# Operands of TensorE given their own start offset in SBUF for each stage of a two-block transformer kernel

## The chip, the cores and the metric

The kernel runs on one core of one Trainium2 chip. The metric is the device time of one execution in microseconds, the median of the runs shown.

## The reference

256 tokens with 1024 features go through three layers, each an attention mixer followed by a gated feed-forward block. All of it is float32.

```python
for i in range(DEPTH):                      # DEPTH = 2
    hn = rmsnorm(x, attn_norm[i])
    x = x + (mixer_dilated(...) if i % 2 == 0 else mixer_moba(...))   # layer A, layer B
    hn = rmsnorm(x, ffn_norm[i])
    x = x + conv_ffn(hn, ...)               # (silu(gate) * val) @ w_down, D_FF = 2816
# second_block: layer C
h = rms_norm(x, norm1_g[l])
proj = h @ w_in[l]                          # q, k, v, forget gate, conv input, pool input
x = x + concatenate([att, conv, pool]) @ w_out[l]
x = x + (silu(gate) * val) @ w_down[l]
```

Layer A has 16 heads and three dilated windows, so its QKV product is 1024 by 9216; layer B has 16 heads (1024 by 3072), layer C 8 heads with a forget gate, a depthwise convolution and a multi-scale pool beside them.

## The kernel before

Every large product is made of three products of float32r operands (a rounded format of 32 bits): each float32 operand is split into a rounded high part and the remainder, and high times high, high times low and low times high are added up in PSUM. The weights, 369 chunks of up to 128 x 1024 values, are streamed from memory in the order of use into a ring of six slots (RING = 6). For each chunk ScalarE writes the high part `w_hi` (L390, function split_hi) and VectorE the low part `w_lo` (L398, split_lo). `w_lo(c)` starts `lo_at(c)` values into its slot's buffer, which is 64 values (STAGGER) longer than a chunk.

The activations are split in the same way: `xg` holds eight tiles of 256 high and 256 low values for the normed input (L483 on ScalarE, L495 on VectorE), `mix_hi` and `mix_lo` the output of the mixer (L984, L1043, L1123, L1156), `g_hi` and `g_lo` two buffers of the gated hidden tile (L1790, L1841).

TensorE works through this program in order:

- QKV units (unit_chunk_pe, L678 to L680; the first chunks early_chunk_pe, L612): 128 tokens of `xg` are the stationary operand and 384 columns of `w_hi` or `w_lo` the moving one; 128 x 3 such matmuls in layer B, three times as many in A, half in C (the first unit of C has 392 columns). Attention of the pair of heads before is put between them.
- output projection (out_pe, L1236 to L1238): weights stationary, 256 columns of `mix_hi` or `mix_lo` moving.
- feed-forward block (ffn_pe, 22 hidden tiles): up projection with 512 moving columns (`xg` high and low together, L430) and 256 (L432), and down projection, 256 columns of `g_hi` or `g_lo` (L1760 to L1762). Sixteen of the tiles run in a loop of eight turns with two tiles each.
- ahead of layer C six input projections (pre_pe, project_k, L416 to L418).

The order on every engine is written out by hand, and counting semaphores tie the engines together. In SBUF each buffer starts where the one before it ends, rounded up to 32 bytes; `w_raw0` starts at byte 16512 of a partition, and small unused buffers (`par_gap`, `gap`, `g_gap`, `cv_gap`) and two pairs of small ones stand between the others and so set where these start.

Of the kernel before, what the change touches and what calls it, by code (L numbers as in the profile page):

```python
# [42 lines left out]
X0 = GAINS  # L43
GAP = 24
STAGGER = 64
LO_UP, LO_DOWN = 16, 32
# [127 lines left out]
def build(nc, x_d, xa_d, stream_d, par_d, con_d, taps_d, out_d):  # L174
# [29 lines left out]
    sb("gap", [P, GAP])  # L204
# [25 lines left out]
    fg_n, fg_l = [sb(f"fg{n}", [P, 2 * HEADS_C]) for n in range(4, 6)]  # L230
# [197 lines left out]
    def project2_k(eng, c, b, k):  # L428
        s = c % RING
        nc.tensor.matmul(bank(b, 0, 2 * TOK), w_hi[s][:, k * P:(k + 1) * P], xg[:, k, :, :].rearrange("p h t -> p (h t)"),  # L430
                         start=(k == 0), stop=False, skip_group_check=True)
        last = nc.tensor.matmul(bank(b), w_lo(c)[:, k * P:(k + 1) * P], xg_hi[:, k, :], start=False,  # L432
                                stop=(k == KT - 1), skip_group_check=True)
        if k == KT - 1:
            last.then_inc(tiles, 1)

    def project2(eng, c, per, i, b):
        eng.wait_ge(w_lo_done, at(c + 1, per, i))
        for k in range(KT):
            project2_k(eng, c, b, k)  # L440

    def project_first(eng, c, b0, b1, e, lag):

        for k in range(KT + lag):
            if k < KT:
                if k == 0:
                    eng.wait_ge(w_lo_done, c + 1)
                eng.wait_ge(x_lo, KT * e + k + 1)
                project2_k(eng, c, b0, k) if e % 2 else project_k(eng, c, bank(b0), xg_hi, xg_lo, k)
            if k >= lag:  # L450
                if k == lag:
                    eng.wait_ge(w_lo_done, c + 2)
                    if e % 2:
                        eng.wait_ge(x_new, KT * (e - 1) + 4)
                project2_k(eng, c + 1, b1, k - lag) if e % 2 else project_k(eng, c + 1, bank(b1), xg_hi, xg_lo, k - lag)
        if e % 2:
            rows_pe(eng, e)
# [11 lines left out]
    def first_hi_dve(eng):  # L469
        eng.wait_ge(x_first, 16)  # L470
        nc.vector.tensor_scalar(xg_hi[:, 0, :], xT[:, 0, :], norm_gain(0, 0), None, ALU.mult).then_inc(x_hi, 1)

    def resid_act(eng, e, m):
        if e == 0:
            x_landed(eng, m)
            if m == 1:
                eng.wait_ge(x_first, 16)
                eng.wait_ge(x_hi, 1)
        else:
            eng.wait_ge(x_new, KT * (e - 1) + m + 1)  # L480
# [10 lines left out]
    def resid_dve_lo(eng, e, m):  # L491
        eng.wait_ge(x_hi, KT * e + m + 1)
        if e == 0:
            x_landed(eng, m)
        nc.vector.scalar_tensor_tensor(xg_lo[:, m, :], xT[:, m, :], norm_gain(e, m), xg_hi[:, m, :].bitcast(F32),  # L495
                                       ALU.mult, ALU.subtract).then_inc(x_lo, 1)
# [106 lines left out]
    def early_chunk_pe(eng, st, n):  # L603
# [5 lines left out]
        def term(x, part, kk, start=False, ends=False):  # L609
            k = 2 * q + kk  # L610
            for t in range(2):
                last = nc.tensor.matmul(bank(unit_bank(st, u, t), 0, UNIT), xg[:, k, x, t * P:(t + 1) * P],  # L612
                                        part[:, kk * UNIT:(kk + 1) * UNIT], start=start, stop=ends)
                if ends and t == 0:
                    last.then_inc(att[st].unit, 1)
            return last
# [27 lines left out]
    def unit_chunk_pe(eng, st, n):  # L644
# [25 lines left out]
        for kk in range(2):  # L670
            k = 2 * q + kk
            wh, wl = w_hi[s][:, kk * width:(kk + 1) * width], w_lo(c)[:, kk * width:(kk + 1) * width]
            if st < 2 and u == 0:
                eng.wait_ge(x_lo, KT * 2 * st + k + 1)
            for t in range(2):
                out = bank(unit_bank(st, u, t), 0, width)
                hi, lo = xg[:, k, 0, t * P:(t + 1) * P], xg[:, k, 1, t * P:(t + 1) * P]
                nc.tensor.matmul(out, hi, wh, start=(k == 0), stop=False)  # L678
                nc.tensor.matmul(out, hi, wl, start=False, stop=False)  # L679
                last = nc.tensor.matmul(out, lo, wh, start=False, stop=(k == KT - 1))  # L680
                if k == KT - 1 and t == 0:
                    last.then_inc(a.unit, 1)
# [295 lines left out]
    def mix_a_act(eng, pr):  # L978
        a = att[0]
        eng.wait_ge(a.pv, pr + 1)  # L980
        if joint(pr):
            unit_wait(eng, 0, joint_unit(pr), 1)
            eng.wait_ge(a.nm, 4 * (pr + 2) + 2)
        nc.scalar.activation(mix_place(mix_hi[:, pr, :]), pv_read(pr), ACT.Copy).then_inc(a.ohi, 1)  # L984
# [55 lines left out]
    def mix_act(eng, st, pr):  # L1040
        a = att[st]
        eng.wait_ge(a.pv, pr + 1)
        nc.scalar.activation(mix_hi[:, pr, :], bank(K_BANK), ACT.Copy).then_inc(a.ohi, 1)  # L1043
# [76 lines left out]
    def mix_a_dve(eng, pr):  # L1120
        a = att[0]
        eng.wait_ge(a.ohi, pr + 1)
        nc.vector.tensor_tensor(mix_place(mix_lo[:, pr, :]), pv_read(pr), mix_place(mix_hi[:, pr, :]).bitcast(F32),  # L1123
# [29 lines left out]
    def mix_dve(eng, st, pr):  # L1153
        a = att[st]
        eng.wait_ge(a.ohi, pr + 1)
        nc.vector.tensor_tensor(mix_lo[:, pr, :], bank(K_BANK), mix_hi[:, pr, :].bitcast(F32), ALU.subtract).then_inc(a.olo, 1)  # L1156
# [57 lines left out]
    def out_pe(eng, st, idx, ms=range(KT)):  # L1214
# [19 lines left out]
        for m in ms:  # L1234
            wh, wl = w_hi[s][:, m * P:(m + 1) * P], w_lo(c)[:, m * P:(m + 1) * P]
            nc.tensor.matmul(out_acc(m), wh, mix_hi[:, k, :], start=(idx == 0 and m % 2 == 0), stop=False, skip_group_check=True)  # L1236
            nc.tensor.matmul(out_acc(m), wh, mix_lo[:, k, :], start=False, stop=False, skip_group_check=True)  # L1237
            last = nc.tensor.matmul(out_acc(m), wl, mix_hi[:, k, :], start=False, stop=(idx == KT - 1), skip_group_check=True)  # L1238
# [501 lines left out]
    def ffn_pe(f):  # L1740
        e = 2 * f + 1

        def step(eng, j, per, i):
            F, b, c, cp = ffn[f], j % 2, ffn_chunk(f, j), 3 * per
            if i is not None or j < FT:
# [3 lines left out]
                else:  # L1749
                    project2(eng, c, cp, i, 2 * b)  # L1750
                    project2(eng, c + 1, cp, i, 2 * b + 1)
                c += 2
            if i is not None or j >= 2:
# [3 lines left out]
                for m in range(KT):  # L1757
                    wh, wl = w_hi[s][:, m * P:(m + 1) * P], w_lo(c)[:, m * P:(m + 1) * P]
                    first = i is None and j == 2 and m % 2 == 0
                    nc.tensor.matmul(acc(m), wh, g_hi[b][:], start=first, stop=False, skip_group_check=True)  # L1760
                    nc.tensor.matmul(acc(m), wh, g_lo[b][:], start=False, stop=False, skip_group_check=True)  # L1761
                    last = nc.tensor.matmul(acc(m), wl, g_hi[b][:], start=False, stop=True, skip_group_check=True)  # L1762
# [10 lines left out]
    def ffn_act(f):  # L1773
        def step(eng, j, per, i):
# [10 lines left out]
            if i is not None or 0 <= t < FT:  # L1785
# [4 lines left out]
                nc.scalar.activation(g_hi[t % 2][:], gated, ACT.Copy).then_inc(F.ghi, 1)  # L1790
# [17 lines left out]
    def ffn_dve(f):  # L1808
        def step(eng, j, per, i):
# [81 lines left out]
    def pre_pe(eng):  # L1891
        project_first(eng, C_PRE, PRE_BANK[0], PRE_BANK[1], 4, 1)
        for n in range(2, N_PRE):
            project(eng, C_PRE + n, 0, None, bank(PRE_BANK[n]), xg_hi, xg_lo)
# [181 lines left out]
    def pool_mix_act(eng):  # L2076
        eng.wait_ge(pool_pe, 1)
        for t in range(2):
            nc.scalar.activation(mix_hi[:, 6 + t, :], bank(Q_BANK, t * TOK), ACT.Copy,
                                 scale=par[:, PAR_PSC + t:PAR_PSC + t + 1]).then_inc(pool_hi, 1)  # L2080

    def pool_mix_dve(eng):
        eng.wait_ge(pool_hi, 2)
        for t in range(2):
            nc.vector.scalar_tensor_tensor(mix_lo[:, 6 + t, :], bank(Q_BANK, t * TOK), par[:, PAR_PSC + t:PAR_PSC + t + 1],
                                           mix_hi[:, 6 + t, :].bitcast(F32), ALU.mult, ALU.subtract).then_inc(side_lo, 1)
# [10 lines left out]
    def conv_mix_act(eng):  # L2097
        eng.wait_ge(ln_pe, 3)
        for o in range(2):
            nc.scalar.activation(mix_hi[:, 4 + o, :], bank(PW_BANK, o * TOK), ACT.Copy).then_inc(ln_act, 1)  # L2100

    def conv_mix_dve(eng):
        eng.wait_ge(ln_act, 6)
        for o in range(2):
            nc.vector.tensor_tensor(mix_lo[:, 4 + o, :], bank(PW_BANK, o * TOK), mix_hi[:, 4 + o, :].bitcast(F32),
# [317 lines left out]
```

## Time and profile before

| | us |
|---|---|
| median of 3 runs | 1039.65 |
| lowest, highest | 1039.22, 1039.83 |
| the profiled execution, its own time | 1039.65 |
| its span | 1037.8 |
| TensorE busy (matmuls) | 1032.0, 99% |
| VectorE busy | 868.2, 84% |
| ScalarE busy | 688.1, 66% |
| GpSimd busy | 354.1, 34% |

The span goes from the first to the last instruction in the trace. A matmul's own length in the trace overlaps the next matmul's, so what a matmul costs is the distance from its start to the next start, taken from the timeline. A timeline row gives start, length, engine, line, operation, what it writes and what it reads (moving operand first, then the stationary one), and the shape.

### The profile page before, as it was taken

What the parts mean: (1) busy time and instruction counts of PE and PEld (TensorE: products, weight loads), DVE (VectorE), ACT (ScalarE), POOL (GpSimd) and SP (SyncE); (2) the same over time, 40 slices, a digit from 0 to 9 for tenths busy, and PEclk for the clock granted to TensorE, in tenths of its full rate; (3) what the DMA queues carried; (4) which work ended last, traced back from release to release, by engine and by line L of the source; (5) the groups of instructions that cost most, each with busy time, mean ns of one, the idle gap of its engine ahead of it and who ended that gap; (6) DMA issues with size and microseconds to landing.
All of it is one profiled execution on the core that took longest, in us unless ns stands there. A gap on an engine that the chain in (4) does not pass through costs nothing.

```text
span 1037.8 us, 21191 instructions
## 1 busy us (share of the span) xinstructions
PE 1032.0 (99%) x7496; PEld 962.3 (93%) x7496; DVE 868.2 (84%) x1589; ACT 688.1 (66%) x1264; POOL 354.1 (34%) x370
## 2 busy tenths in 40 slices
PE   9999999999999999999999999999999999999998
PEld 8999999999999999999999899999988998999998
DVE  7877778777799988887777999988896769999886
ACT  7766777766766655576776766665686667666563
POOL 5222222112256433332111556333350015653332
PEclk9999999999999999999999999999999999999999
DMA  9654454456476665535453566656534536666651
GB/s 317 231 164 156 148 173 160 147 172 205 160 223 212 201 194 187 179 104 186 155 175 133 187 204 218 194 190 191 159 107 135 161 123 203 204 212 193 199 163 41
DMA packets 57749, 183.34 MB, mean 177 GB/s; under 512 B 6352, under 2 KB 9680, under 8 KB 57424
## 3 DMA queue, kind: packets, MB, share of 16 engines
q1 hardware_dynamic: 56816, 181.52, 54.0%
q10 hardware_dynamic: 864, 0.92, 0.3%
q8 instruction: 41, 0.67, 0.3%
q14 instruction: 28, 0.23, 0.1%
HBM read 181.36 MB, written 1.05 MB: 176 GB/s over the span
## 4 chain that ended last, share of the span: by engine, by line
PE 94%; DVE 5%; DMA 0%; issue 0%; ACT 0%; DVEq 0%
PE ps L430 20%; PE ps L432 10%; PE ps L678 10%; PE ps L680 9%; PE ps L679 9%; PE ps L1760 6%; PE ps L1762 6%; PE ps L1761 6%; DVE w_lo L398 2%; PE ps L1236 2%; PE ps L1238 2%; PE ps L1237 2%; PE ps L612 1%; PE ps L856 1%; PE ps L901 1%; PE ps L830 1%
## 5 line engine op out<-in xcount | busy, mean ns | idle before, releaser
L398 DVE TENSOR_TENSOR w_lo<-w_raw,w_hi 128x1024 fp32r<-128x1024 f32 (+2 forms) x369 | 442.0, 1214 | 32.6 <-ACT w_hi L390 31.9
L390 ACT ACTIVATE w_hi<-w_raw 128x1024 fp32r<-128x1024 f32 (+2 forms) x369 | 353.5, 972 | 125.7 <-PE ps L432 108.6
L430 PE MATMUL ps<-xg,w_hi 128*128 128x512 f32 x1056 | 364.3, 391 | 0.8 <-DVE xg L495 0.6
L432 PE MATMUL ps<-xg,w_lo 128*128 128x256 f32 x1056 | 291.7, 276 | 0.0
L430 PEld LDWEIGHTS ps<-xg,w_hi 128*128 128x128 f32 x1056 | 198.2, 188 | 41.7 <-DVE xg L495 2.9
L432 PEld LDWEIGHTS ps<-xg,w_lo 128*128 128x128 f32 x1056 | 198.2, 188 | 0.1
L1882 POOL TENSOR_TENSOR prob_t<-prob_t,qkT 128x256 f32<-128x256 f32 x63 | 104.5, 1659 | 261.8 <-ACT prob_t L1805 261.8
L678 PE MATMUL ps<-w_hi,xg 128*128 128x384 f32 (+1 forms) x556 | 192.3, 346 | 0.0
L680 PE MATMUL ps<-w_hi,xg 128*128 128x384 f32 (+1 forms) x556 | 187.4, 337 | 0.0
L679 PE MATMUL ps<-w_lo,xg 128*128 128x384 f32 (+1 forms) x556 | 185.6, 334 | 0.0
L1760 PE MATMUL ps<-g_hi,w_hi 128*128 128x256 f32 x528 | 146.2, 277 | 0.5 <-DVE g_lo L1841 0.3
L1761 PE MATMUL ps<-g_lo,w_hi 128*128 128x256 f32 x528 | 145.9, 276 | 0.0
L1762 PE MATMUL ps<-g_hi,w_lo 128*128 128x256 f32 x528 | 145.8, 276 | 0.0
L1876 POOL TENSOR_TENSOR qkT<-prob,rms_r 128x256 f32<-128x256 f32 x132 | 125.9, 974 | 18.5 <-ACT rms_r L543 10.7
L1852 DVE SCALAR_TENSOR_TENSOR qkT<-qkT,par 128x255 f32<-128x255 f32 (+1 forms) x264 | 112.3, 478 | 6.5 <-ACT qkT L1798 6.5
L1798 ACT ACTIVATE qkT<-qkT,par 128x256 f32<-128x256 f32 x132 | 78.2, 598 | 50.5 <-POOL qkT L1876 48.8
L678 PEld LDWEIGHTS ps<-w_hi,xg 128*128 128x128 f32 x556 | 104.2, 187 | 3.3 <-issue 2.7
L680 PEld LDWEIGHTS ps<-w_hi,xg 128*128 128x128 f32 x556 | 104.5, 188 | 0.0
L679 PEld LDWEIGHTS ps<-w_lo,xg 128*128 128x128 f32 x556 | 104.3, 188 | 0.1
L1760 PEld LDWEIGHTS ps<-g_hi,w_hi 128*128 128x128 f32 x528 | 99.1, 188 | 3.7 <-issue 1.3
L1762 PEld LDWEIGHTS ps<-g_hi,w_lo 128*128 128x128 f32 x528 | 99.1, 188 | 0.0
L1761 PEld LDWEIGHTS ps<-g_lo,w_hi 128*128 128x128 f32 x528 | 99.1, 188 | 0.0
(191 smaller groups left out, 1389.6 us busy)
## 6 DMA issues: line engine op xcount, KB each, us to landing
w_raw<-w_stream SPq DMA_DIRECT2D x228, 512.0 KB, 4.0
w_raw<-w_stream SPq DMA_DIRECT2D x137, 384.0 KB, 3.3
w_raw<-w_stream SPq DMA_DIRECT2D x4, 392.0 KB, 3.1
con<-consts SPq DMA_DIRECT2D x1, 1024.0 KB, 7.1
x_all<-x_t SPq DMA_DIRECT2D x4, 256.0 KB, 5.3
conv_taps<-taps SPq DMA_DIRECT2D x1, 1024.0 KB, 7.7
w_raw<-w_stream SPq DMA_DIRECT2D x4, 192.0 KB, 4.6
x_all<-x_a SPq DMA_DIRECT2D x3, 256.0 KB, 5.5
```

Of the source, the lines that this page charges most:

```text
L390: nc.scalar.activation(w_hi[s][:, 0:w], w_raw[s][:, 0:w], ACT.Copy).then_inc(w_hi_done, 1)
L398: nc.vector.tensor_tensor(w_lo(c)[:, 0:w], w_raw[s][:, 0:w], w_hi[s][:, 0:w].bitcast(F32), ALU.subtract).then_inc(w_lo_done, 1)
L430: nc.tensor.matmul(bank(b, 0, 2 * TOK), w_hi[s][:, k * P:(k + 1) * P], xg[:, k, :, :].rearrange("p h t -> p (h t)"), start=(k == 0), stop= ...
L432: last = nc.tensor.matmul(bank(b), w_lo(c)[:, k * P:(k + 1) * P], xg_hi[:, k, :], start=False, stop=(k == KT - 1), skip_group_check=True)
L678: nc.tensor.matmul(out, hi, wh, start=(k == 0), stop=False)
L679: nc.tensor.matmul(out, hi, wl, start=False, stop=False)
L680: last = nc.tensor.matmul(out, lo, wh, start=False, stop=(k == KT - 1))
L1760: nc.tensor.matmul(acc(m), wh, g_hi[b][:], start=first, stop=False, skip_group_check=True)
L1761: nc.tensor.matmul(acc(m), wh, g_lo[b][:], start=False, stop=False, skip_group_check=True)
L1762: last = nc.tensor.matmul(acc(m), wl, g_hi[b][:], start=False, stop=True, skip_group_check=True)
L1852: nc.vector.scalar_tensor_tensor(cv_s[b][s][:, k:TOK], up_s[b][s][:, 0:TOK - k], par_col(f, t, per, i, 4 * s + 2 - k), cv_s[b][s][:, k:TOK ...
L1876: nc.gpsimd.tensor_tensor(up_s[t % 2][s], up_sum[s], rms_r[:], ALU.mult).then_inc(F.up, 1)
```

## The change

Buffers that TensorE reads may now start at an offset that depends on the stage. One buffer `xg_all` holds six overlapping views `xg[e]`, one for each normed input e (0, 2 and 4 for the QKV products of A, B and C, 1, 3 and 5 for the feed-forward blocks); `mix_hi`, `mix_lo`, `g_hi` and `g_lo` get a view for each layer; `lo_at` has an offset of its own for each kind of chunk. Each function that reads or writes these buffers takes the view of its stage. The gaps between buffers are resized. No instruction is added, removed or moved to another place in its engine's order, no shape changes, and semaphores and DMAs stay as they are.

```diff
-X0 = GAINS
-GAP = 24
-STAGGER = 64
-LO_UP, LO_DOWN = 16, 32
+X0 = 64
+GAP = 184
+SHIFT = 32
+X_AT = (16, 16, 8, 16, 16, 16)
+G_AT = ((8, 8), (8, 8), (8, 8))
+MIX_AT = ((16, 16), (16, 16), (16, 48))
+LO_QKV, LO_OUT, LO_PRE, LO_UP, LO_DOWN = (16, 0, 16), (0, 0, 16), 0, 16, 0
...
 def lo_at(c):
     for f in range(3):
         if c < OUT_C0[f]:
-            return LO_DOWN if f == 2 and c < C_QKV else LO_UP
+            return LO_PRE if f == 2 and c < C_QKV else LO_QKV[f]
         if c < FFN_C0[f]:
-            return LO_DOWN
+            return LO_OUT[f]
...
-    w_low = [sb(f"w_lo{s}", [P, CHUNK + STAGGER], F32R) for s in range(RING)]
+    w_low = [sb(f"w_lo{s}", [P, CHUNK + SHIFT], F32R) for s in range(RING)]
...
-    xg = sb("xg", [P, KT, 2, TOK], F32R)
-    xg_hi, xg_lo = xg[:, :, 0, :], xg[:, :, 1, :]
-    fg_r, fg_x = [sb(f"fg{n}", [P, 2 * HEADS_C]) for n in range(2)]
-    mix_hi = sb("mix_hi", [P, KT, TOK], F32R)
-    mix_lo = sb("mix_lo", [P, KT, TOK], F32R)
-    fg_m, fg_e = [sb(f"fg{n}", [P, 2 * HEADS_C]) for n in range(2, 4)]
-    sb("par_gap", [P, 16])
+    xg_all = sb("xg", [P, KT * 2 * TOK + SHIFT], F32R)
+    xg = [xg_all[:, o:o + KT * 2 * TOK].rearrange("p (k h t) -> p k h t", h=2, t=TOK) for o in X_AT]
+    xg_hi, xg_lo = [x[:, :, 0, :] for x in xg], [x[:, :, 1, :] for x in xg]
+    mix_all = [sb(f"mix_{n}", [P, KT * TOK + 2 * SHIFT], F32R) for n in ("hi", "lo")]
+    mix_hi, mix_lo = [[mix_all[n][:, o[n]:o[n] + KT * TOK].rearrange("p (k t) -> p k t", t=TOK) for o in MIX_AT]
+                      for n in range(2)]
...
-    sb("gap", [P, GAP])
+    sb("gap", [P, GAP - 5 * SHIFT])
...
-    fg_n, fg_l = [sb(f"fg{n}", [P, 2 * HEADS_C]) for n in range(4, 6)]
+    fg_r, fg_x, fg_m, fg_e, fg_n, fg_l = [sb(f"fg{n}", [P, 2 * HEADS_C]) for n in range(6)]
...
-    sb("g_gap", [P, 8])
-    g_hi = [sb(f"g_hi{b}", [P, TOK], F32R) for b in range(2)]
-    g_lo = [sb(f"g_lo{b}", [P, TOK], F32R) for b in range(2)]
-    sb("cv_gap", [P, 24])
+    g_all = sb("g_hi0", [P, 4 * TOK + SHIFT], F32R)
+    g_hi, g_lo = [[[g_all[:, o[n] + (2 * n + b) * TOK:o[n] + (2 * n + b + 1) * TOK] for b in range(2)] for o in G_AT]
+                  for n in range(2)]
...
-    def project2_k(eng, c, b, k):
+    def project2_k(eng, c, e, b, k):
...
-                hi, lo = xg[:, k, 0, t * P:(t + 1) * P], xg[:, k, 1, t * P:(t + 1) * P]
+                hi, lo = xg[2 * st][:, k, 0, t * P:(t + 1) * P], xg[2 * st][:, k, 1, t * P:(t + 1) * P]
...
-                    nc.tensor.matmul(acc(m), wh, g_hi[b][:], start=first, stop=False, skip_group_check=True)
+                    nc.tensor.matmul(acc(m), wh, g_hi[f][b], start=first, stop=False, skip_group_check=True)
```

All other edits of the diff put the stage's index in where these buffers are read or written. From the sizes of the buffers, the first bytes of the operands in a partition, as remainders of 256, are:

| operand | before | after |
|---|---|---|
| w_hi, every slot | 128 | 128 |
| w_lo, QKV of A and C, and up projections | 192 | 192 in even slots, 64 in odd ones |
| w_lo, QKV of B | 192 | 128 even, 0 odd |
| w_lo, output projection of A and B, input projections, down projections | 0 | 128 even, 0 odd |
| w_lo, output projection of C | 0 | 192 even, 64 odd |
| xg, all stages but the QKV of B | 192 | 192 |
| xg, QKV of B | 192 | 160 |
| mix_hi; mix_lo in A and B | 64 | 64 |
| mix_lo in C | 64 | 192 |
| g_hi, g_lo | 192 | 192 |
| x_all (the residual, xT) | 192 | 128 |

The slots of `w_lo` are 4352 bytes apart before and 4224 after. The buffers from `par` to `tri` lie 256 bytes lower than before, and those from `cv_h0` on where they were.

## Rows read from the trace of the kernel before

**Rows 1.** The page: span, busy time of each engine, TensorE's granted clock.
```profile
span 1037.8 us, 21191 instructions
PE 1032.0 (99%) x7496; PEld 962.3 (93%) x7496; DVE 868.2 (84%) x1589; ACT 688.1 (66%) x1264; POOL 354.1 (34%) x370
...
PEclk9999999999999999999999999999999999999999
```

**Rows 2.** The waits of TensorE: total us, how many, longest.
```profile
PE ps L2165 <- DVE zero L2217: 1.1, 1, 1.1
PE ps L430 <- DVE xg L495: 0.6, 2, 0.3
PE ps L1760 <- DVE g_lo L1841: 0.3, 2, 0.2
```

**Rows 3.** The page's costliest groups: busy us, mean ns of one, idle before.
```profile
L398 DVE TENSOR_TENSOR w_lo<-w_raw,w_hi 128x1024 fp32r<-128x1024 f32 (+2 forms) x369 | 442.0, 1214 | 32.6 <-ACT w_hi L390 31.9
...
L430 PE MATMUL ps<-xg,w_hi 128*128 128x512 f32 x1056 | 364.3, 391 | 0.8 <-DVE xg L495 0.6
...
L678 PE MATMUL ps<-w_hi,xg 128*128 128x384 f32 (+1 forms) x556 | 192.3, 346 | 0.0
```

**Rows 4.** Timeline of TensorE, up projection of block 1: start us, length us.
```profile
316.10 0.39 PE L430 MATMUL ps<-xg,w_hi 128*128 128x512 f32 x1
...
317.12 0.39 PE L430 MATMUL ps<-xg,w_hi 128*128 128x512 f32 x1
```

**Rows 5.** Timeline of TensorE, down projection, ring slot 5, first pass.
```profile
301.12 0.28 PE L1761 MATMUL ps<-g_lo,w_hi 128*128 128x256 f32 x1
...
303.85 0.39 PE L430 MATMUL ps<-xg,w_hi 128*128 128x512 f32 x1
```

**Rows 6.** The same lines and slot one pass later.
```profile
317.46 0.28 PE L1760 MATMUL ps<-g_hi,w_hi 128*128 128x256 f32 x1
...
320.18 0.39 PE L430 MATMUL ps<-xg,w_hi 128*128 128x512 f32 x1
```

**Rows 7.** Timeline of TensorE, QKV products of layer A.
```profile
119.72 0.34 PE L680 MATMUL ps<-w_hi,xg 128*128 128x384 f32 x1
...
121.79 0.34 PE L680 MATMUL ps<-w_hi,xg 128*128 128x384 f32 x1
```

**Rows 8.** Timeline of TensorE, QKV products of layer B.
```profile
495.20 0.34 PE L680 MATMUL ps<-w_hi,xg 128*128 128x384 f32 x1
...
496.77 0.34 PE L680 MATMUL ps<-w_hi,xg 128*128 128x384 f32 x1
```

**Rows 9.** Timeline of TensorE, first QKV unit of layer C, 392 columns.
```profile
770.15 0.34 PE L678 MATMUL ps<-w_hi,xg 128*128 128x392 f32 x1
...
771.23 0.34 PE L678 MATMUL ps<-w_hi,xg 128*128 128x392 f32 x1
...
772.30 0.34 PE L678 MATMUL ps<-w_hi,xg 128*128 128x392 f32 x1
```

**Rows 10.** Timeline of TensorE, input projections ahead of layer C.
```profile
757.40 0.28 PE L418 MATMUL ps<-xg,w_lo 128*128 128x256 f32 x1
...
760.97 0.28 PE L418 MATMUL ps<-xg,w_lo 128*128 128x256 f32 x1
...
764.03 0.28 PE L416 MATMUL ps<-xg,w_hi 128*128 128x256 f32 x1
...
770.04 0.28 PE L418 MATMUL ps<-xg,w_lo 128*128 128x256 f32 x1
```

**Rows 11.** Timeline of TensorE, output projection of layer C.
```profile
838.71 0.28 PE L1236 MATMUL ps<-mix_hi,w_hi 128*128 128x256 f32 x1
...
842.45 0.28 PE L1236 MATMUL ps<-mix_hi,w_hi 128*128 128x256 f32 x1
```

**Rows 12.** Windows: busy us of PE, PEld, DVE, ACT, POOL; clock; DMA.
```profile
456.10:569.10 113.00, 113.00 (x791) 105.57 (x790) 86.27 (x230) 81.87 (x206) 24.40 (x42) 1.00 0.48 157
569.10:751.10 182.00, 181.42 (x1237) 166.60 (x1236) 167.99 (x235) 115.38 (x171) 80.19 (x70) 1.00 0.59 190
```

More of the change, by code:

```diff
@@ L425, in project @@
             project_k(eng, c, out, hi, lo, k)
-    def project2_k(eng, c, b, k):
+    def project2_k(eng, c, e, b, k):
         s = c % RING
-        nc.tensor.matmul(bank(b, 0, 2 * TOK), w_hi[s][:, k * P:(k + 1) * P], xg[:, k, :, :].rearrange("p h t -> p (h t)"),
+        nc.tensor.matmul(bank(b, 0, 2 * TOK), w_hi[s][:, k * P:(k + 1) * P], xg[e][:, k, :, :].rearrange("p h t -> p (h t)"),
                          start=(k == 0), stop=False, skip_group_check=True)
-        last = nc.tensor.matmul(bank(b), w_lo(c)[:, k * P:(k + 1) * P], xg_hi[:, k, :], start=False,
+        last = nc.tensor.matmul(bank(b), w_lo(c)[:, k * P:(k + 1) * P], xg_hi[e][:, k, :], start=False,
                                 stop=(k == KT - 1), skip_group_check=True)
@@ L1122, in mix_a_dve @@
         eng.wait_ge(a.ohi, pr + 1)
-        nc.vector.tensor_tensor(mix_place(mix_lo[:, pr, :]), pv_read(pr), mix_place(mix_hi[:, pr, :]).bitcast(F32),
+        nc.vector.tensor_tensor(mix_place(mix_lo[0][:, pr, :]), pv_read(pr), mix_place(mix_hi[0][:, pr, :]).bitcast(F32),
                                 ALU.subtract).then_inc(a.olo, 1)
@@ L1155, in mix_dve @@
         eng.wait_ge(a.ohi, pr + 1)
-        nc.vector.tensor_tensor(mix_lo[:, pr, :], bank(K_BANK), mix_hi[:, pr, :].bitcast(F32), ALU.subtract).then_inc(a.olo, 1)
+        nc.vector.tensor_tensor(mix_lo[st][:, pr, :], bank(K_BANK), mix_hi[st][:, pr, :].bitcast(F32), ALU.subtract).then_inc(a.olo, 1)
     def gains_dve(eng):
@@ L1235, in out_pe @@
             wh, wl = w_hi[s][:, m * P:(m + 1) * P], w_lo(c)[:, m * P:(m + 1) * P]
-            nc.tensor.matmul(out_acc(m), wh, mix_hi[:, k, :], start=(idx == 0 and m % 2 == 0), stop=False, skip_group_check=True)
-            nc.tensor.matmul(out_acc(m), wh, mix_lo[:, k, :], start=False, stop=False, skip_group_check=True)
-            last = nc.tensor.matmul(out_acc(m), wl, mix_hi[:, k, :], start=False, stop=(idx == KT - 1), skip_group_check=True)
+            nc.tensor.matmul(out_acc(m), wh, mix_hi[st][:, k, :], start=(idx == 0 and m % 2 == 0), stop=False, skip_group_check=True)
+            nc.tensor.matmul(out_acc(m), wh, mix_lo[st][:, k, :], start=False, stop=False, skip_group_check=True)
+            last = nc.tensor.matmul(out_acc(m), wl, mix_hi[st][:, k, :], start=False, stop=(idx == KT - 1), skip_group_check=True)
             if idx == KT - 1 and m < KT - 1:
@@ L1759, in step @@
                     first = i is None and j == 2 and m % 2 == 0
[L1760 to L1762 removed]
+                    nc.tensor.matmul(acc(m), wh, g_hi[f][b], start=first, stop=False, skip_group_check=True)
+                    nc.tensor.matmul(acc(m), wh, g_lo[f][b], start=False, stop=False, skip_group_check=True)
+                    last = nc.tensor.matmul(acc(m), wl, g_hi[f][b], start=False, stop=True, skip_group_check=True)
                     if m == KT - 1:
@@ L2104, in conv_mix_dve @@
         for o in range(2):
-            nc.vector.tensor_tensor(mix_lo[:, 4 + o, :], bank(PW_BANK, o * TOK), mix_hi[:, 4 + o, :].bitcast(F32),
+            nc.vector.tensor_tensor(mix_lo[2][:, 4 + o, :], bank(PW_BANK, o * TOK), mix_hi[2][:, 4 + o, :].bitcast(F32),
                                     ALU.subtract).then_inc(side_lo, 1)
```

38 lines of the change are left out of this document (19 added, 19 removed).

## Prediction

> **What bounds the kernel now.** I read the page first. TensorE is busy 1032.0 of the 1037.8 us of the span, at the full granted clock (2.4 GHz) in all 40 slices [rows 1]. Then its waits: the listed ones are 1.1, 0.6 and 0.3 us [rows 2], so no other engine holds it up by more than about 2 us in all. So a change of addresses can pay only in one way: the distance from one matmul's start to the next has to change. It can cost in that way too, or by making VectorE or ScalarE so slow that TensorE has to wait for them.
>
> So I looked at distances in the timeline, and set them against the columns streamed at 2.4 GHz. In the up projection three pairs of 512 and 256 columns take 1.02 us, 340 ns a pair [rows 4]; 768 columns at 2.4 GHz are 320 ns. In the down projection, one pass of ring slot 5 takes 24 matmuls from 317.46 to 320.18, 113.3 ns each [rows 6]; 256 columns are 106.7 ns. Both are 17/16 of the column time. Call the added part the sixteenth. The reader is to see that it grows with the columns (20 ns on 768, 6.7 on 256), so it isn't a fixed cost of an instruction.
>
> On top of the sixteenth there is a second, smaller excess. The same lines, the same ring slot and so the same addresses took 23 matmuls from 301.12 to 303.85 one pass earlier, 118.7 ns each [rows 5]: 5.4 ns more. The input projections ahead of layer C do the same: 30 matmuls in 3.57 us, 119.0 ns each, and later 53 in 6.01 us, 113.4 ns [rows 10]. The QKV products always have some: in A 12 matmuls in 2.07 us, 172.5 ns [rows 7], in B 9 in 1.57 us, 174.4 ns [rows 8], where 384 columns with the sixteenth are 170.0. That one address pair shows both 113.3 and 118.7 says that how two streams of reads meet in time matters here, and that the start address alone doesn't decide it.
>
> **The change part by part.** The sum starts at the profiled execution, 1039.65 us, which is also the median. No instruction, wait or DMA is added or moved, so each engine issues what it did; the terms are differences of rate.
>
> Feed-forward blocks. The remainders of `xg` and `g` stay at 192, `w_hi` stays at 128, and `w_lo` moves by 128 bytes in one half of the slots. These lines already run at 340 ns a pair and 113.3 ns [rows 4, 6], so nothing above the sixteenth is left to win. The bounds are 0 below, and above 5.4 ns for every matmul that meets a moved `w_lo` (priced as a rival). I take 0: before, `w_lo` stands at 192 in the up and at 0 in the down projection, and both run at the same 17/16.
>
> QKV of layer A and C. `xg` stays, `w_lo` moves by 128 in the odd slots. From below, half of A's 1152 matmuls could lose their 2.5 ns, 1.4 us; from above nothing is known that is worse than the 5.4 ns of [rows 5]. I take 0, for the same reason.
>
> QKV of layer B. This is the one stage where an operand leaves the 64-byte grid: `xg` goes from 192 to 160, `w_lo` from 192 to 128 or 0. The nearest rows are those of C's first unit. Its matmuls have 392 columns, so the second half of each chunk starts 1568 bytes on, 32 bytes off that grid, while `xg` stays on it. Six matmuls on the grid take 1.08 us, 180.0 ns, and the six off it 1.07 us, 178.3 ns [rows 9]. So the distance is 1.7 ns smaller there, on the moving side instead of the stationary one. B has 384 such matmuls: 384 x 1.7 ns = 0.6 us less. The bounds: all of the excess gone, 384 x (174.4 - 170.0) = 1.7 us less; or the rate of C's aligned rows, 180.0 x 384/392 = 176.3 ns, 384 x 1.9 = 0.7 us more. I take -0.6, the row.
>
> Output projections and input projections. Layer C's output projection runs at 3.74 us for 33 matmuls, 113.3 ns [rows 11], and has nothing to win; `mix_lo` and `w_lo` move there, and 192 matmuls at 5.4 ns would cost 1.0 us. The input projections could win 5.6 ns on about 90 matmuls, 0.5 us [rows 10]. I take 0 for both.
>
> VectorE and ScalarE. They now write `w_lo`, `xg` and `mix_lo` at other starts, and read `x_all` at 128 for 192. L398 has 369 instructions of 1214 ns on average [rows 3], with starts of 192 and 0 mixed among them, and I found no difference that goes with the start. Should they become slower anyway, the cover is this: VectorE is busy 167.99 of 182.00 us in a feed-forward block [rows 12], 14 us of room over 66 chunks, 0.2 us a chunk. Beyond that `w_lo` would be late and TensorE would wait. I cost it at nothing.
>
> The sum is 1039.65 - 0.6 = 1039.0 us.
>
> The slow pass of [rows 5] can be read against a rule: the Trainium skill, "SBUF — State Buffer", section "Who interferes with whom", gives TensorE two independent read ports, one for the moving operand and one for loading weights, and says that it waits for no other engine. By it placement would be worth nothing anywhere, and the time would be 1039.65. The rows do show 5.4 ns that come and go at one address, which the rule doesn't explain; so it speaks against this change and doesn't exclude it.
>
> **The rivals.** First, the excess over the sixteenth depends on the placement after all, and the new one is the better. B would give all of 1.7 us, A and C the half whose `w_lo` moved (1.4 us, and 96 matmuls x 3 ns = 0.3 us in C), the input projections 0.5 us: 3.9 us, so 1035.7. For it speaks that A and B, with the same code, keep an excess of 2.5 to 4.4 ns all the way [rows 7, 8]; against it that rows 5 and 6 differ at one address, and that the moved operands in the feed-forward blocks have no excess to lose.
>
> Second, on the other side: the new distances of 128 bytes between `w_lo` and `xg` or `g` in the odd slots hold the chip in the slow mode of [rows 5]. What meets the moved `w_lo` while it is loaded is L430 (1056, half of them in odd slots, 528) and L1761 (528, half 264): 792 x 5.4 ns = 4.3 us, so 1043.9. It decides against the kernel from 385 matmuls in that mode (2.08 us). For it speaks that no pair in the trace stands 128 bytes apart, so nothing shows it harmless; against it that distances of 0, 64 and 192 all run clean.
>
> Third, the sixteenth itself hangs on the 64-byte grid. Then B, off it, would stream 384 columns in 160.0 ns: 384 x (174.4 - 160.0) = 5.5 us less, 1034.1. Against it speak the 392-column rows, off the grid and not free of it (178.3 against 163.3 ns of columns) [rows 9]. The Trainium skill, "TensorE: Matmul & The Clock Gate", section "Back-to-back issue gap", gives columns over 2.4 plus about 2.5 ns for a warm matmul, 162.5 ns here; the trace has 174.4, and by that rule the same stage would give 4.6 us.
>
> **How the numbers follow.** The measurement of this kernel can tell about 0.2%, 2.08 us, from no change. The forecast, all terms within 2 us, gets 0.59, and its own range is 1037.6 to 1041.7. The first rival gets 0.21, the third 0.06, so faster has 0.27. The second gets 0.14. The range leaves out the second and the third (0.20), goes down to the first's 1035.7, and up to the edge of no change, 1041.8.
>
> **What the changed kernel's profile would show.** If I'm right, pairs of L430 and L432 stay at 340 ns and the down projection at 113.3 ns in even and in odd slots, B's L678 to L680 stay between 170 and 176 ns, and instruction counts are the same on each engine. If the first rival is right, the mean distance in B falls to 170; if the third, to about 160. If the second is right, the odd slots of the feed-forward blocks show 5 ns more a matmul than the even ones. The prediction would be wrong if matmuls in stages whose remainders didn't move ran at another distance, which would mean that whole addresses count and not remainders, or if a wait of TensorE for VectorE of over 2 us turned up.

## The result, and the profile after

The changed kernel is slower: 1047.05 us median of 4 runs (1046.88 to 1047.63) against 1039.73 (4 runs, 1039.22 to 1039.83), a ratio of 1.0073 (95% interval 1.0055 to 1.0090). That is 7.3 us more. I had forecast 1039.0 in a range of 1035.7 to 1041.8.

The page after; the rows of before are [rows 1] and [rows 3]:

```profile
span 1044.8 us, 21191 instructions
PE 1039.9 (100%) x7496; PEld 970.0 (93%) x7496; DVE 865.2 (83%) x1589; ACT 687.6 (66%) x1264; POOL 348.1 (33%) x370
...
PEclk9999999999999999999999999999999999999999
...
L398 DVE TENSOR_TENSOR w_lo<-w_raw,w_hi 128x1024 fp32r<-128x1024 f32 (+2 forms) x369 | 442.5, 1214 | 41.7 <-ACT w_hi L390 41.4
```

The span grew by 7.0 us and TensorE's busy time by 7.9, with the same counts of instructions, the same clock, and 1214 ns for L398 as before. The other engines are no busier. TensorE's waits (total, times, longest) have become shorter; the two for `xg` and `g_lo` of [rows 2] are gone:

```profile
PE ps L2165 <- DVE zero L2217: 1.1, 1, 1.1
PE ps L612 <- ACT w_hi L405: 0.3, 1, 0.3
```

So the loss is in the distances between matmuls. Below is the timeline of TensorE in layer A's feed-forward block (start, length), to be set beside [rows 4] and [rows 6]: the first row of each of five groups of 16 or 24 matmuls, and of the one behind them. A pair is one matmul of L430 and one of L432.

```profile
307.93 0.40 PE L430 MATMUL ps<-xg,w_hi 128*128 128x512 f32 x1
...
310.72 0.28 PE L1760 MATMUL ps<-g_hi,w_hi 128*128 128x256 f32 x1
...
313.54 0.39 PE L430 MATMUL ps<-xg,w_hi 128*128 128x512 f32 x1
...
316.32 0.39 PE L430 MATMUL ps<-xg,w_hi 128*128 128x512 f32 x1
...
319.05 0.28 PE L1760 MATMUL ps<-g_hi,w_hi 128*128 128x256 f32 x1
...
321.77 0.39 PE L430 MATMUL ps<-xg,w_hi 128*128 128x512 f32 x1
```

In order these are: an up chunk in ring slot 1, 2.79 us for 8 pairs, 349 ns a pair; the down projection in slot 2, 2.82 us for 24, 117.5 ns each; up chunk in slot 3, 2.78 us, 348 ns; up chunk in slot 4, 2.73 us, 341; down projection in slot 5, 2.72 us, 113.3. Before, a pair took 340 and a down matmul 113.3. The up chunks in odd slots are slow (`w_lo` at 64) and those in even slots (192) are as before, to 0.01 us a chunk; and of the down projections the one that comes behind a slow up chunk is slow. Below, a group is called clean if it runs at 17/16 of its column time, and slow if it runs some ns a matmul above that; its rhythm is the distance that repeats in it.

For totals I take each distance between starts in the packed trace, which has them in whole ns, subtract 17/16 of the column time, and sum; distances over 1.15 of the column time plus 5 ns count as pauses. In us:

| | before | after | difference |
|---|---|---|---|
| up projections | 0.5 | 4.5 | +4.0 |
| down projections | 0.4 | 3.6 | +3.2 |
| QKV of A, B, C | 5.6 | 7.6 | +2.0 |
| output projections | 0.7 | 1.2 | +0.5 |
| pauses in the up projections | 4.2 | 1.8 | -2.4 |
| all else, with all other pauses | 18.6 | 18.4 | -0.2 |
| sum | 30.0 | 37.0 | +7.0 |

The difference of the sums is the difference of the spans. The down projections' term is three blocks of 10 passes, 720 matmuls, at 4.4 ns: 3.2 us. The QKV products go from 172.5 ns [rows 7] to 175.0 for the same 12 matmuls of layer A (over the whole stage, without pauses, the mean goes from 173.4 to 174.9):

```profile
120.35 0.34 PE L680 MATMUL ps<-w_hi,xg 128*128 128x384 f32 x1
...
122.45 0.34 PE L680 MATMUL ps<-w_hi,xg 128*128 128x384 f32 x1
```

and layer C's output projection from 113.3 [rows 11] to 118.5 for 33 matmuls, while the input projections took 113.7 ns for 30 where they took 119.0 [rows 10]:

```profile
762.62 0.28 PE L418 MATMUL ps<-xg,w_lo 128*128 128x256 f32 x1
...
766.03 0.28 PE L418 MATMUL ps<-xg,w_lo 128*128 128x256 f32 x1
...
843.98 0.28 PE L1236 MATMUL ps<-mix_hi,w_hi 128*128 128x256 f32 x1
...
847.89 0.28 PE L1236 MATMUL ps<-mix_hi,w_hi 128*128 128x256 f32 x1
```

### The profile page after: what moved, and what is told of

It is laid out like the page before. It is cut to its first block, busy times and chain, and to the rows that moved or that the text cites. A ratio compares the mean times of both kernels' runs of the same rounds, so it can differ in the third digit from the quotient of the medians.

```text
span 1044.8 us, 21191 instructions
## 1 busy us (share of the span) xinstructions
PE 1039.9 (100%) x7496; PEld 970.0 (93%) x7496; DVE 865.2 (83%) x1589; ACT 687.6 (66%) x1264; POOL 348.1 (33%) x370
## 4 chain that ended last, share of the span: by engine, by line
PE 99%; DMA 0%; DVE 0%; ACT 0%; issue 0%; DVEq 0%
PE ps L430 23%; PE ps L432 12%; PE ps L678 10%; PE ps L680 9%; PE ps L679 9%; PE ps L1760 6%; PE ps L1762 6%; PE ps L1761 6%; PE ps L1236 2%; PE ps L1238 2%; PE ps L1237 2%; PE ps L612 1%; PE ps L856 1%; PE ps L901 1%; PE ps L830 1%; PE ps L868 1%
## 5 line engine op out<-in xcount | busy, mean ns | idle before, releaser
L398 DVE TENSOR_TENSOR w_lo<-w_raw,w_hi 128x1024 fp32r<-128x1024 f32 (+2 forms) x369 | 442.5, 1214 | 41.7 <-ACT w_hi L390 41.4
L430 PE MATMUL ps<-xg,w_hi 128*128 128x512 f32 x1056 | 367.4, 391 | 0.0
L432 PE MATMUL ps<-xg,w_lo 128*128 128x256 f32 x1056 | 293.5, 278 | 0.0
L430 PEld LDWEIGHTS ps<-xg,w_hi 128*128 128x128 f32 x1056 | 198.4, 188 | 40.9 <-DVE xg L495 0.2
L432 PEld LDWEIGHTS ps<-xg,w_lo 128*128 128x128 f32 x1056 | 198.0, 187 | 0.1
L1760 PE MATMUL ps<-g_hi,w_hi 128*128 128x256 f32 x528 | 147.1, 279 | 0.3
L1761 PE MATMUL ps<-g_hi,w_hi 128*128 128x256 f32 x528 | 146.6, 278 | 0.0
L1876 POOL TENSOR_TENSOR qkT<-prob,rms_r 128x256 f32<-128x256 f32 x132 | 122.0, 945 | 18.5 <-ACT rms_r L543 7.0
L1760 PEld LDWEIGHTS ps<-g_hi,w_hi 128*128 128x128 f32 x528 | 99.1, 188 | 3.6 <-issue 1.2
L1761 PEld LDWEIGHTS ps<-g_hi,w_hi 128*128 128x128 f32 x528 | 98.9, 187 | 0.0
```

Of the source, the lines that this page charges most:

```text
L398: nc.vector.tensor_tensor(w_lo(c)[:, 0:w], w_raw[s][:, 0:w], w_hi[s][:, 0:w].bitcast(F32), ALU.subtract).then_inc(w_lo_done, 1)
L1760: nc.tensor.matmul(acc(m), wh, g_hi[f][b], start=first, stop=False, skip_group_check=True)
L1761: nc.tensor.matmul(acc(m), wh, g_lo[f][b], start=False, stop=False, skip_group_check=True)
L1876: nc.gpsimd.tensor_tensor(up_s[t % 2][s], up_sum[s], rms_r[:], ALU.mult).then_inc(F.up, 1)
```

## The experiments

Diffs are against the kernel before where nothing else is said. An offset is in values of 4 bytes, a place is the remainder of the first byte by 256. "Excess" is the distance above 17/16 of the column time, mean of a group. Where a kernel ran once, its time is that one run.

### Which part of the change costs

**e1_pitch: the slots' distance alone.** `w_lo` slots 4224 bytes apart for 4352.

```diff
-    w_low = [sb(f"w_lo{s}", [P, CHUNK + STAGGER], F32R) for s in range(RING)]
+    w_low = [sb(f"w_lo{s}", [P, CHUNK + STAGGER // 2], F32R) for s in range(RING)]
+    sb("w_lo_pad", [P, RING * STAGGER // 2])
```

> The kernel before with one thing of the change: the slots of w_lo 4224 bytes apart for 4352, an unused buffer after them keeping all else in place. Theory: the start of w_lo as a remainder of 256, set against the operands it is used with, makes the loss, so the odd slots alone slow down: half of 2112 up-projection matmuls by 3.7 ns (3.9 us), half of 1584 down-projection ones by 4.4 ns (3.5 us), about 1 us more in the QKV products: 1047 to 1048 us. Rival: the moved xg and w_lo of layer B and the moved mix_lo of C carry it: then this one is at 1040 us.

Measured 1049.08 us (1048.79 to 1049.26), ratio 1.0090 (1.0073 to 1.0107). Up +4.0, down +4.0, QKV +2.2 us, where the changed kernel has +4.0, +3.2 and +2.0. The shorter slots carry the whole loss, and more than it: of the pauses only 0.8 us went, for 2.4.

**e13_no_pitch: all the rest.** The slots stay 4352 bytes apart; every other place that the change gives is kept, and `w_lo` stands at 128 or 192 in all slots as the changed kernel has it in even ones. x_all stays at 192.

```diff
-            return LO_DOWN if f == 2 and c < C_QKV else LO_UP
+            return 0 if f == 2 and c < C_QKV else (16, 0, 16)[f]
...
-            return LO_DOWN
+            return (0, 0, 16)[f]
...
-    xg = sb("xg", [P, KT, 2, TOK], F32R)
+    X_AT = (0, 0, 56, 0, 0, 0)
```

> The change without its new slot size: slots of w_lo 4352 bytes apart as before, and all else as in the even slots of the change: xg of layer B at 160, w_lo at 128 in B, in the output projections of A and B, in the input and down projections, at 192 in C, mix_lo of C at 192. Theory: the loss comes through the odd slots alone, so about 0.7 us is left of it in the output projection of C: 1040.4 us. Rival: these parts carry 2 us or more: 1042 us and up.

Measured 1039.19 us (10 runs, 1038.97 to 1039.40), ratio 0.9995 (0.9985 to 1.0005): no change. Up chunks and down projections are clean again.

**e2_qkv_b: the edit of layer B's QKV alone**, the one I had put at -0.6 us (`xg` at 160, `w_lo` at 128 in every slot, where the change has 0 in the odd ones).

> The kernel before with the change in layer B's QKV products alone: xg 32 bytes lower, w_lo at remainder 128 (one value in all slots, where the change has 128 and 0). The changed kernel's stage B has 174.5 ns where the one before has 173.6: 384 matmuls, 0.3 us more, 1040.0 us. Rival from the prediction: 0.6 us less, 1039.1 us; read in the trace, since the runs can't tell them apart.

1039.71 us. The mean distance in B goes from 173.5 to 173.9 ns, about 0.1 us more on 384: neither my -0.6 nor either bound is seen.

**e7_all_128: all buffers 128 bytes on**, by one unused buffer ahead of `w_raw0`.

```diff
+    sb("front", [P, 32])
```

> The kernel before with an unused buffer of 128 bytes ahead of w_raw0, so that every buffer starts 128 bytes later. If the distance between the operands counts, nothing changes: 1039.7 us. If the start of w_lo itself counts (64 bad in the up, 128 bad in the down projection), all slots of both are slow: 7.8 and 7.0 us more, 1054.5 us.

1040.59 us. The span is 1.0 us longer, most of it in pauses of the QKV products (+1.1), and the down projections stay clean, the up projections within 0.4 us. So moving all operands together by 128 bytes costs next to nothing: what counts is how they stand to each other.

### Up and down projections apart

**e3_down_128** and **e4_up_64** move `w_lo` in one kind of chunk only: to 128 for 0 in the down projections, to 64 for 192 in all the up projections.

```diff
-            return LO_DOWN if j >= 6 and j % 3 == 0 or j >= 3 * FT - 2 else LO_UP
+            return 0 if j >= 6 and j % 3 == 0 or j >= 3 * FT - 2 else LO_UP          # e3
+            return LO_DOWN if j >= 6 and j % 3 == 0 or j >= 3 * FT - 2 else 48       # e4
```

> The kernel before, slots 4352 bytes apart, with w_lo at remainder 128 for 0 in the down projections, in every slot. Theory of the remainder: all 1584 down-projection matmuls take 4.4 ns more, 7.0 us, so 1046.7 us, and the up projections stay at 340 ns a pair. Rival, the distance between the slots (4224 for 4352 bytes) is what counts: 1039.7 us.

> The kernel before, slots 4352 bytes apart, with w_lo at remainder 64 for 192 in the up projections, in every slot. Theory of the remainder: 2112 matmuls take 3.7 ns more on average, 7.8 us, so 1047.5 us, and the down projections stay at 113.3 ns. Rival, the distance between the slots counts: 1039.7 us.

e3 1039.57 us: 128 bytes more in the down projection cost nothing. e4 1053.50 us, 13.7 more: the excess of the up projections grows by 6.5 us, and that of the down projections, whose operands all stand where they stood, by 8.4 us (5.6 ns on every matmul). The slots of e4 are 4352 bytes apart as before, so it is the place of `w_lo` that costs and not the distance between slots.

**e14_first_64** and **e15_second_64** put 64 in only the first or only the second of a tile's two up chunks; the second comes right ahead of the down projection.

```diff
+            second = (j % 2 if j < 6 else j % 3 == 2)
+            return LO_UP if second else 48      # e14; e15: return 48 if second else LO_UP
```

> The kernel before with w_lo at remainder 64 for 192 in the first of the two up chunks of each hidden tile, the one after the down projection. Theory of inheritance: the second up chunk, at 192, falls back into the fast rhythm and hands it to the down projection, so only the first chunk's 1056 matmuls pay 3.5 ns each, 3.7 us: 1043.4 us. Rival, one slow chunk is enough to spoil the tile: up to 1055 us.

> The same in the second of the two up chunks, the one ahead of the down projection. Theory of inheritance: 3.7 us for the chunk itself and 5.6 ns for each of 1584 down-projection matmuls, 8.8 us: 1052 us. Rival, the down projection isn't tied to the chunk ahead of it: 1043.4 us, as with the first chunk.

e14 1043.56 us, e15 1051.44 us: the same number of chunks at 64, and 7.9 us between them. The timeline of e14, TensorE:

```profile
312.09 0.40 PE L433 MATMUL ps<-xg,w_hi 128*128 128x512 f32 x1
...
314.87 0.39 PE L433 MATMUL ps<-xg,w_hi 128*128 128x512 f32 x1
...
317.60 0.28 PE L1763 MATMUL ps<-g_hi,w_hi 128*128 128x256 f32 x1
...
320.32 0.40 PE L433 MATMUL ps<-xg,w_hi 128*128 128x512 f32 x1
```

and of e15:

```profile
306.94 0.40 PE L433 MATMUL ps<-xg,w_hi 128*128 128x512 f32 x1
...
309.72 0.28 PE L1763 MATMUL ps<-g_hi,w_hi 128*128 128x256 f32 x1
...
312.57 0.39 PE L433 MATMUL ps<-xg,w_hi 128*128 128x512 f32 x1
...
315.31 0.40 PE L433 MATMUL ps<-xg,w_hi 128*128 128x512 f32 x1
```

In e14 the slow chunk takes 2.78 us, the clean chunk behind it 2.73, the down projection 2.72. In e15 the slow chunk (2.78) stands ahead of the down projection, which then takes 2.85; the up chunk behind that one is clean again, 2.74. A down projection takes over the slow rhythm that `w_lo` at 64 makes, and an up chunk with `w_lo` at 192 doesn't. That is shown for these places; why is not.

The start of layer A's block shows that places aren't all, in the kernel before itself. Its up chunks from 281.08 to 292.46, slots 4, 5, 0 and 1, run at 350 ns a pair with `w_lo` at 192; up chunks in slots 0, 1 and 4 are clean on every later pass of that block. Here is the one in slot 1, 2.80 us for 8 pairs:

```profile
289.66 0.40 PE L430 MATMUL ps<-xg,w_hi 128*128 128x512 f32 x1
...
292.46 0.28 PE L1760 MATMUL ps<-g_hi,w_hi 128*128 128x256 f32 x1
```

The same four chunks are slow in e7 and e18 and clean in e2, e16 and e17, and the first pass in slot 5 [rows 5] is slow in before and e7 and clean in those four others, with the places of these operands to each other the same in all six. Each time a pause of TensorE lies right ahead, in or before the first matmuls of the group. So after a pause either rhythm can come up at the places of before; in these six kernels a slow one lasts for four groups at most. Why the one or the other comes up is open.

### Looking for a rule, and for better places

**e8_after_up0: the changed kernel with `w_lo` at 128 and 0 in the up projections** (`LO_UP` 0 for 16). My first theory after the result was that a distance of 128 bytes to `xg` alone was to blame.

> The changed kernel with one constant of it altered: LO_UP 0 for 16, so that w_lo starts at remainder 128 in even and 0 in odd slots of the up projections, 64 bytes below and above the remainder 192 of xg, and nowhere 128 bytes from it. Theory: the loss comes from the up projections where xg streams while w_lo is loaded from 128 bytes off, and the down projection that follows such a chunk only inherits the slow rhythm; then both are cured, 3.9 and 3.2 us less, about 1040 us. Rival, the down projections are slow through their own operands (which stay as in the changed kernel): 3.9 us less at most, 1043 us, with slot 2 of block 1 still at 4.4 ns over.

1054.99 us (1054.96 to 1055.12), ratio 1.0144 (1.0127 to 1.0161): 8 us worse than the change. The theory falls. `w_lo` 64 bytes below `xg`'s place or 64 above it is slow as well; all up chunks, in even and odd slots, and all but one of the 66 down passes are slow.

**e5_map_w_lo: another start of `w_lo` for nearly every slot and block** of the feed-forward blocks, with `xg` at 192.

> A map: the kernel before with another start of w_lo in each slot and block, so that the trace of one run shows the up projections at twelve distances between w_lo and xg. Theory: distance 0 is at 340 ns a pair, distance 128 slow, and between them the cost rises; the down projection follows the up chunk ahead of it whatever its own offset. Rival: anything off the 64-byte grid is slow, or everything but 128 is clean. The time is somewhere between 1040 and 1050 us.

1052.19 us. Excess of the two matmuls of a pair (L430 and L432 of the kernel before) in ns by the place of `w_lo`: 0: 2.4, 4.4; 32: 5.3, 3.4; 64: 2.8, 5.8; 96: 4.3, 4.8; 128: 5.5, 5.4; 144: 1.9, 5.0; 160: 4.2, 4.2; 176: 5.0, 8.3; **192: 0.7, 0.0**; 208: 1.8, 1.0; 224: 1.7, 5.0; 240: 5.8, 7.5. Only the place of before is clean, and 16 bytes more already cost. What runs ahead of a chunk differs from place to place here, so a single value can hold some of its neighbour's rhythm.

**e9_pair_64, e10_g_moved, e6_map_moving** move the moving operands: `xg` and `w_lo` both to 64; `g_hi` and `g_lo` to 160, 224 and 0 in the three blocks; in e6 `g` so, and `xg` to 224, 0 and 64.

```diff
+    X_AT = (0, 32, 0, 32, 0, 32)      # e9, with w_lo offset 48 in the up projections
+    G_AT = (0, 16, 24)                # e10
+    X_AT = (0, 8, 0, 16, 0, 32)       # e6, with G_AT as in e10
```

> The kernel before with xg and w_lo of the feed-forward blocks both moved by 128 bytes, to remainder 64, and w_hi left at 128. If only the distance between w_lo and xg counts (0, as before), nothing changes: 1039.7 us. Rival, the distance between w_hi and xg counts too (now 64 above, before 64 below): the up projections are slow by 3 to 4 ns a matmul and the down projections with them, 13 to 15 us, 1054 us.

> The kernel before with g alone moved, to remainders 160, 224 and 0 in the three blocks. Theory: the down projection keeps the rhythm of the up projection ahead of it, whatever its own operands' places, so nothing changes: 1039.7 us. Rival, its own operands count as well (they did not where w_lo went from 0 to 128): one or more blocks at 4 to 5 ns over in the down projection, 2.3 us a block, up to 1047 us.

> The kernel before with the streamed operand moved and w_lo left alone: xg at remainder 224, 0 and 64 in the three feed-forward blocks, g at 160, 224 and 0. If the distance between xg and w_lo counts (32, 64 and 128 bytes), the third block is the slow one, by 5 us, and the second is clean; the place of g changes nothing: 1044 to 1045 us. If the start of w_lo alone counts, nothing changes: 1039.7 us.

e9 1047.71, e10 1048.05, e6 1054.27 us. In e9 the up projections are nearly clean (0.4 to 1.2 ns, means of a block) with `xg` and `w_lo` together at 64. The down projections are slow in e9 and in e10 (5.0 to 5.5 ns) behind clean up chunks. In e10 only `g` moved, so the down projection's own operands count too. In e9 none of its operands moved, and the chunk ahead is clean: what it takes over from the up chunk isn't only a slow rhythm, the place of `xg` there matters as well. How is open. I had expected e10 and e6 far too low: in both I had put the place of `g` at nothing.

**e11_after_plain** and **e12_all_equal**: the changed kernel with all `w_lo` slots at 192; and `w_hi`, `w_lo` and `xg` all at 128.

```diff
-    w_low = [sb(f"w_lo{s}", [P, CHUNK + SHIFT], F32R) for s in range(RING)]     # e11
+    sb("w_lo_front", [P, 16])
+    w_low = [sb(f"w_lo{s}", [P, CHUNK], F32R) for s in range(RING)]
+    sb("w_lo_back", [P, RING * SHIFT - 16])
...
+    X_AT = (48,) * 6                  # e12, with w_lo offset 0 everywhere
```

> The changed kernel with w_lo in plain slots of 4096 bytes, all starting at remainder 192, the remainder of xg in the feed-forward blocks; the xg of layer B and mix_lo of C stay as changed. Theory: distance 0 is restored in the up projections, so the up and down projections are back at 340 and 113.3 ns, and the QKV products of A and C too: 6.5 us less than the changed kernel, 1040.3 us. Rival, the distance between slots (4352 bytes before, 4096 here) matters by itself: it stays above 1043 us.

> The kernel before with xg and w_lo moved to remainder 128 in all stages, the remainder of w_hi, so that all three are at distance 0. If distance 0 is what makes a pair clean, the QKV products may lose their excess too (5.6 us): 1034 us. If only w_lo against xg counts, it is 1039.7 us. If a distance of 64 between w_hi and xg is needed, the up projections turn slow: 1054 us.

e11 1046.61 us (1046.17 to 1048.39), ratio 1.0068 (1.0054 to 1.0082). Its up chunks are clean, and its down projections take 2.83 us each, 117.9 ns, with `w_lo` at 192 where 0 and 128 were clean:

```profile
306.92 0.39 PE L432 MATMUL ps<-xg,w_hi 128*128 128x512 f32 x1
...
309.64 0.28 PE L1762 MATMUL ps<-g_hi,w_hi 128*128 128x256 f32 x1
...
312.47 0.39 PE L432 MATMUL ps<-xg,w_hi 128*128 128x512 f32 x1
```

e12 1052.27 us (1052.10 to 1052.69), ratio 1.0119 (1.0104 to 1.0135). Equal places of `xg` and `w_lo` don't do if `w_hi` stands there too: its up projections have 3.6 to 6.1 ns a matmul, by block. Its down projections in slot 5 of layer A are clean behind such a chunk, so a slow chunk ahead isn't always taken over.

**e16_map_qkv: twelve other starts of `w_lo` in the QKV products of A and B.**

```diff
+            return LO_DOWN if f == 2 and c < C_QKV else ((0, 8, 24, 32, 40, 48), (56, 4, 12, 20, 28, 36), (16,) * 6)[f][c % RING]
```

> A map of the QKV products: the kernel before with another start of w_lo in each slot of A (0, 8, 24, 32, 40, 48 values) and of B (56, 4, 12, 20, 28, 36), for 16. The excess over 17/16 is 3.5 ns a matmul now. Theory: no start gives less, 16 is the best and 48 (distance 128 from xg) costs 5.5: 1040 to 1042 us. Rival: some start brings it near 0, which would be worth up to 5.6 us in all stages.

1041.72 us. Excess between 4.4 (place 32) and 7.7 ns (176), where the same chunks have 3.1 to 4.2 with `w_lo` at 192. 192 is the best of thirteen there too, and no start of `w_lo` removes the rest.

### The gain that went with the loss

The pauses that became shorter stand mostly at the starts of the feed-forward blocks of B and C, 1.0 to 1.2 us each, in the changed kernel and in e13. The rows are those of L495, which writes the low part of `xg`, around B's start (565 to 578 us): busy, mean ns. Before, after, and e17 (which is described below):

```profile
L495 DVE SCALAR_TENSOR_TENSOR xg<-x_all,par,xg 128x256 fp32r<-128x256 f32 x8 | 5.6, 712 | 0.2 <-ACT xg L483 0.2
```

```profile
L495 DVE SCALAR_TENSOR_TENSOR xg<-x_all,par,xg 128x256 fp32r<-128x256 f32 x8 | 4.9, 619 | 0.3 <-ACT xg L483 0.2
```

```profile
L495 DVE SCALAR_TENSOR_TENSOR xg<-x_all,par,xg 128x256 fp32r<-128x256 f32 x8 | 4.8, 599 | 0.3 <-ACT xg L483 0.2
```

In the timeline of before five of the eight overlap L513 on GpSimd by 0.5 to 0.7 us (for example 570.06 to 571.06, with L513 from 570.04 to 570.78), and take 0.71 to 1.00 us; in e13 the four that overlap it by 0.3 us or less take 0.47 to 0.55.

**e17_out_ab** puts `w_lo` at 128 for 0 in the output projections of A and B; **e18_out_all** also at 192 in that of C, and at 128 in the input projections.

```diff
-            return LO_DOWN
+            return (0, 0, LO_DOWN)[f]         # e17; e18: (0, 0, 16)[f]
```

> Only w_lo in the output projections of layers A and B moves, from remainder 0 to 128, as in e13_no_pitch and in the changed kernel. Theory: the starts of feed-forward blocks B and C lose about 2.4 us of TensorE's pauses in e13_no_pitch because of this edit: the output projection runs in another rhythm, so VectorE's L495 falls beside GpSimd's L513 less often (mean of eight 600 ns for 711). Layer B's output projection feeds the block at 568 us, so 1.2 us of that goes here; the block behind C's output projection keeps its pauses. 1039.7 - 1.2 + at most 0.3 for the output projection itself: 1038.6. Rival: the edit has nothing to do with it and the shorter pauses come from the place of the buffers mix_lo, fg2 and fg3: 1039.7 to 1040.0, L495 at 711 ns as before.

> As e17_out_ab, and w_lo in layer C's output projection at 192 for 0 and in the six input projections ahead of C at 128 for 0, with mix_lo left where it is. Theory: both starts lose their 1.2 us, C's output projection pays about 0.4 us at 192 (13 groups of matmuls at 3 ns), the input projections 0.3: 1038.0. Rival (buffers, not w_lo): 1040.4, with L495 at 711 ns at 568 us and pauses as before at 854 us.

e17: 1039.16 us (11 runs), ratio 0.9996 (0.9987 to 1.0005); L495 599 ns at B's start and 710 at C's; the pauses 1.1 us shorter at B's and unchanged at C's. e18: 1039.34 us, 0.9995 (0.9986 to 1.0004), 598 and 595 ns, both starts shorter, and the output and input projections 1.4 us longer. So it is the place of `w_lo` in the output projection ahead. All twenty kernels agree: behind an output projection with `w_lo` at 0, L495 has a mean of 709 to 712 ns at the start of B's and C's blocks (so too in e1, with 128 in the odd slots alone), and behind one with it moved in the even slots, 595 to 620. That this goes by the moment at which VectorE's work meets GpSimd's is read from the timelines; no run moves that moment by itself. Neither e17 nor e18 is measurably faster than the kernel before, and no version here beats it.

## Why the prediction was wrong

**The step that failed** is "Feed-forward blocks. [...] I take 0: before, `w_lo` stands at 192 in the up and at 0 in the down projection, and both run at the same 17/16." The rows were read rightly and the conclusion was wrong. Two places that both run clean, each with its own moving operand, say nothing of a third; e5, e11 and e4 show that 192 is right in the up and wrong in the down projection, and that 64 is wrong in the up projection. From "nothing above the sixteenth is left to win" it should have followed that every edit here could only cost, so the odds were not even. The blocks cost 4.0 + 3.2 us where I had 0. I had also overlooked that four up chunks at the start of layer A's block run at 350 ns a pair.

**Rival 2 came nearest to the mechanism, mis-sized.** It named the odd slots, 4.3 us and 1043.9. In the odd slots of the up projection L430 is 2.1 ns over and L432 5.1 ns on average, 528 x 7.2 ns = 3.8 us, where it had 528 x 5.4 = 2.9 us, all on L430. The down projection cost 720 matmuls at 4.4 ns, 3.2 us, for its 264 at 5.4, 1.4 us, since the passes are slow by what stands ahead of them, and in even slots as well as odd: the moved `w_lo` of the down projection, on which it counted, costs nothing (e3). The QKV products it left out. Its ground "distances of 0, 64 and 192 all run clean" fell with e8, e11 and e12: 0 and 64 bytes between `w_lo` and `xg` or `g` are clean in one stage and slow in another. I gave it 0.14.

**QKV of A and C**: "from above nothing is known that is worse than the 5.4 ns", I took 0, "for the same reason". It measured +1.7 us, the same failed inference; e16 shows every other place worse than 192. **QKV of B**: taken at -0.6, measured +0.3. The same 9 matmuls take 173.3 ns for 174.4 [rows 8], but over the stage the mean goes from 173.5 to 174.4. The -0.6 had no ground: 1.08 and 1.07 us over six matmuls [rows 9] differ by one step of the printed hundredths, and the trace has 1079 and 1074 ns, 0.8 ns a matmul for the 1.7.

**Output and input projections**: 0 taken; +0.5 and -0.1 us.

**VectorE and ScalarE**: "I cost it at nothing" was right for their durations and the cover (L398 1214 ns in both), but I looked only for them becoming slower. L495 became shorter, and 2.4 us of pauses went with it; the rows for it were in the waits of L430 for `xg` [rows 2], which list 0.6 us where the distances hold 4.2.

**Rival 1** (a better placement) and **rival 3** (the sixteenth hangs on the 64-byte grid) fell: B, off that grid, stays at 173.9 ns in e2, and 340 ns a pair and 113.3 ns are the floor in all of the kernels. What the sixteenth is stays open.

The rule of independent ports in the Trainium skill, "SBUF — State Buffer", section "Who interferes with whom", would make all of these kernels last as long as the one before. The runs go from 1039.2 to 1055.0 us by addresses alone, with one clock and the same counts, so the measurement decides against using it for placement. The same section's rule that only VectorE and GpSimd share ports agrees with L495 beside L513, 712 against 599 ns; that they share one isn't shown by a run here.

**Open**: which pairs of places are fast, and why; by what the down projection takes over a rhythm; which rhythm comes up after a pause, as in the first pass in slot 5 of [rows 5], slow before and after (5.6 and 5.4 ns over, layer A's block).

## What to carry to other kernels

When TensorE hardly waits and some lines already run at the best distance seen anywhere in the trace, a change of operand addresses has nothing to win there and something to lose: price the loss by the slow rows of the same trace, and give it the odds. Changing the length of a ring's slots changes addresses in every stage that uses the ring, and with one offset for each stage half of the slots stand elsewhere; work out the remainders slot by slot first, or give each slot its own offset, as e5 does. A difference worked out from a few rows printed to 0.01 us can be nothing but rounding: take more rows. Distances from start to start show what the list of waits and the mean lengths of instructions don't.

## What was unexpected of the hardware

- The distance between float32r matmuls depends on the places of operands in a partition, to 16 bytes (e5): 340 ns a pair at best and 348 to 349 in the changed kernel's slow chunks; 113.3 ns a matmul of 256 columns, and 117.5 to 118.8 in slow down projections (after, e15). The placement was worth up to 15.4 us of 1039.6 (e8), 1.4%.
- A matmul whose own operands didn't move becomes 5.5 ns slower by what ran ahead of it (e15, 2.85 for 2.72 us a pass). The same operands at the same places also show both rhythms in one execution, 340 and 350 ns a pair (before, layer A's block).
- The sixteenth, 17/16 of the column time at 2.4 GHz, appeared in each kernel and at no placement went away.
- The place of `w_lo` in TensorE's output projection decides whether L495 on VectorE, behind it, takes 710 or 599 ns (e17); in the timeline the long ones lie beside GpSimd's L513.
